# A hybrid block on one core: early loads of attention's keys in the scan's buffers, waits in pieces, another order in the projection

## The reference

```python
h = modulate(x, shift, scale)                     # from the condition vector c
z, xbc, dt, q, k, v, g = split_projection(h @ w_in)
xbc = silu(depthwise_conv_centred(xbc, w, b))     # 5 taps
# branch A: chunked scan (chunks of 128) in both directions, D_INNER = 2048
y = ssd(x*dt, dt*A, B, C) + reversed + d_skip*x ; y = rms_norm(y * silu(z)) @ w_ssd_br
# branch B: 16 query heads, 4 key heads, head size 64; block of 128 queries reads
# 3 blocks of keys (|i-j| <= 128), a sink logit, and all 256 context keys
q, k = apply_rope(q), apply_rope(k)
a = softmax([q.k_window, q.k_context, sink]) @ v ; a = a @ w_attn_br
x = layer_norm(alpha*x + gate * ((sigmoid(g1)*y + sigmoid(g2)*a) @ w_o))
x = layer_norm(alpha*x + gate * experts(x))       # 16 experts, each picks its tokens
```

## Time and profile before

| | value |
|---|---|
| median of 3 runs (lowest, highest) | 2726.47 us (2726.16, 2729.87) |
| profiled execution | 2728.03 us, span 2726.4 us |
| TensorE busy | 2425.6 us, 89% of the span |
| VectorE busy | 1710.5 us, 63% |
| ScalarE busy | 1090.6 us, 40% |
| GpSimd busy | 484.0 us, 18% |
| DMA | 572.02 MB, mean 210 GB/s |
| mean granted clock of TensorE | 0.944 |

### The profile page before, as it was taken

How to read it: one execution, slowest core, us unless ns; L and a number is a source line. 1 busy time by engine, 2 the same in 40 slices (tenths; PEclk the granted TensorE clock), 3 DMA queues, 4 the chain that set the end, 5 groups by cost and what they waited for, 6 DMA issues and landing times. The chain is left out here.

```text
span 2726.4 us, 32819 instructions
## 1 busy us (share of the span) xinstructions
PE 2425.6 (89%) x12804; PEld 1983.2 (73%) x12804; DVE 1710.5 (63%) x1827; ACT 1090.6 (40%) x1363; POOL 484.0 (18%) x385
## 2 busy tenths in 40 slices
PE   7899999989989996894999969999872899999993
PEld 2788888777788885673666659999661788888882
DVE  5555555444234773783565557674666699999996
ACT  3333332221123111551333454442432577777772
POOL 0000000021003432894000000000343011111112
PEclk8899999999999998996999979999895899999996
DMA  5222234576336865976444269978435699999994
GB/s 217 76 77 79 77 125 108 154 233 224 120 114 211 293 250 175 319 264 171 64 75 99 64 186 263 265 212 226 156 116 224 254 381 404 401 400 397 396 382 139
DMA packets 360756, 572.02 MB, mean 210 GB/s; under 512 B 25014, under 2 KB 269206, under 8 KB 337258
## 3 DMA queue, kind: packets, MB, share of 16 engines
q1 hardware_dynamic: 331610, 464.93, 51.2%
q0 software_dynamic: 23376, 97.36, 11.1%
q10 hardware_dynamic: 5632, 7.87, 1.0%
HBM read 460.09 MB, written 104.49 MB: 207 GB/s over the span
## 5 line engine op out<-in xcount | busy, mean ns | idle before, releaser
L2653 DVE TENSOR_TENSOR e_wlo<-e_w,e_whi 128x2048 fp32r<-128x2048 f32 x188 | 425.4, 2289 | 42.4 <-ACT e_whi L2602 41.1
L2602 ACT CAST e_whi<-e_w 128x2048 fp32r<-128x2048 f32 x192 | 365.3, 1909 | 124.0 <-PE e_gu L2779 83.0
L459 PE MATMUL f_lat<-h_hi,w_hi 128*128 128x512 f32 x800 | 255.1, 400 | 20.5 <-DVE w_lo L610 20.5
L459 PE MATMUL f_lat<-h_lo,w_hi 128*128 128x512 f32 x800 | 252.0, 396 | 0.0
L459 PE MATMUL f_lat<-h_hi,w_lo 128*128 128x512 f32 x800 | 251.9, 396 | 0.0
L2113 PE MATMUL b_acc<-b_hi,b_whi 128*128 128x256 f32 x768 | 219.1, 285 | 7.2 <-issue 7.2
L2113 PE MATMUL b_acc<-b_hi,b_wlo 128*128 128x256 f32 x768 | 218.4, 284 | 0.0
L2113 PE MATMUL b_acc<-b_lo,b_whi 128*128 128x256 f32 x768 | 218.4, 284 | 0.0
L459 PEld LDWEIGHTS f_lat<-h_hi,w_hi 128*128 128x128 f32 x800 | 138.1, 189 | 52.3 <-DVE w_lo L610 20.9
L459 PEld LDWEIGHTS f_lat<-h_lo,w_hi 128*128 128x128 f32 x800 | 140.7, 189 | 30.1
L459 PEld LDWEIGHTS f_lat<-h_hi,w_lo 128*128 128x128 f32 x800 | 140.5, 189 | 30.0
(11 more groups left out here) (375 smaller groups left out, 5416.4 us busy)
## 6 DMA issues: line engine op xcount, KB each, us to landing
e_w<-in_w_gate_up SPq DMA_DIRECT2D x128, 1024.0 KB, 11.0
e_w<-in_w_down SPq DMA_DIRECT2D x64, 1024.0 KB, 9.1
w_raw<-in_w_in SPq DMA_DIRECT2D x50, 512.0 KB, 4.0
t_space<-xbcT POOLq DMA_DIRECT2D x18, 1280.0 KB, 6.3
before<-t_space SPq DMA_DIRECT2D x16, 1024.0 KB, 4.5
y_before<-before SPq DMA_DIRECT2D x64, 256.0 KB, 6.2
l_w<-in_w_ssd_br SPq DMA_DIRECT2D x20, 768.0 KB, 7.3
xbcT<-t_out POOLq DMA_DIRECT2D x20, 640.0 KB, 4.4
```

The costliest lines, as they stand in the source:

```text
L459: mm = nc.tensor.matmul(o, weights[:, b, k, :], part[:, k, a:a + n], start=(k == 0 and n_pass == 0), stop=(k == KT - 1 and n_pass == 2))
L2602: nc.scalar.copy(whi[:, slot % SPLIT], w[:, slot]).then_inc(w_hi, 1)
L2653: V.tensor_tensor(wlo[:, slot % SPLIT], w[:, slot], whi[:, slot % SPLIT].bitcast(F32), ALU.subtract).then_inc(w_split, 1)
```

## The change

**Projection.** `keep_lo` of tile n - 1 stands ahead of `rotate_in` of tile n on VectorE. The gates are written into `padded` (their stores read it), without a wait for the low halves. Of `padded` only three strips at the edges are cleared. The last row of modulation is stored ahead of the last gate tile.

**Scan and attention share one space in SBUF** (class `Early`): the scan's three slots are laid out so that keys, queries and masks fit in a slot when its last chunk is done. SyncE issues the loads for attention's first block behind the stores of units 23 to 30. The ones in k2 and the zeros in q2 come by transfer from a constant `flat` of two long rows. Query blocks 1 and 2, with their zeros, are issued by ScalarE at the start of attention. z, y, `decay` and `pre` of the scan lie in buffers of the later stage (class `Later`, now made ahead of the scan; it was made before attention).

**Scan.** The wait for a chunk's tiles is split into four (`bc_in`, `cum_in`, `group_in` with the table, `rows_in` with the lanes). Nothing but the rows of ones is filled, and the matmuls of the exponents read 18 rows. The constants' loads follow the first bc tiles. The last unit's sums and product are made by VectorE. The wait for the stores of y and the `recycle` after the scan are gone; GpSimd waits for the stores in attention, ahead of `load_branch`.

**Attention.** The memset of v is GpSimd's. The maxima of block 0 wait for mask, identity and edges alone, not for all constants. `maximum` writes its sum in place, in PSUM.

The core of the diff:

```diff
 def constants
+        "flat": np.stack([np.zeros(KVH * KV_TOK, np.float32), np.ones(KVH * KV_TOK, np.float32)]),
...
 project_f_stage, sync: store_gate
-                    sp.dma_start(gF[row:row + P, :], wide[:, n % 2, CTX:TOK]).then_inc(gate_out[n % 2], 16)
+                    sp.dma_start(gF[row:row + P, :], padded[:, n % 2, 0:SEQ]).then_inc(gate_out[n % 2], 16)
                 for n in range(NG - 3, NG):
-                    store_gate(n)
                     if n == NG - 1:
                         for c in range(REST):
                             if c not in [SUM_AFTER[k] for k in SUM_AFTER if k + 4 < NG]:
                                 store_rest(c)
+                    store_gate(n)
 scalar: evacuate, gates
-                        act.wait_ge(qk_lo_made, NQK - 1 + b)
-                        nc.scalar.activation(wide[:, b, CTX:TOK], lat[:, b, :], ACT.Sigmoid).then_inc(acc_free, 1)
+                        nc.scalar.activation(padded[:, b, 0:SEQ], lat[:, b, :], ACT.Sigmoid).then_inc(acc_free, 1)
 vector
-                dve.memset(padded[:], 0.0).then_inc(conv_step, 2 * CS)
+                for a, b in ((0, 2), (2 + CTX, 6 + CTX), (PAD - 2, PAD)):
+                    dve.memset(padded[:, :, a:b], 0.0).then_inc(conv_step, 2 * CS // 3)
                 for n in range(1, NQK):
                     split_lo(NX + n + 2, n % 2)
+                    keep_lo(n - 1)
                     rotate_in(NX + n, n % 2, n)
-                    keep_lo(n - 1)
...
+class Early:
+    def load_query(self, eng, part, rows, out, m):
+        at = KV_LAT0 + m * P
+        eng.dma_start(out[rows].bitcast(F32), part[0:QH * HD, :].rearrange("(h d) t -> d h t", d=HD)[:, :, at:at + P]).then_inc(self.q_in[m], 16)
+    def blank(self, s, eng, m):
+        eng.dma_start(self.q2[m][HD:P].bitcast(F32).rearrange("p h q -> p (h q)"), s.flat[0:1, 0:QH * P].to_broadcast([HD, QH * P])).then_inc(self.q_in[m], 16)
+    def load(self, s, eng, qkH, qkL, u):
+        low, high = slice(0, HD), slice(HD, P)
+        if u == 23:
+            self.load_key(eng, qkH, low, self.k1, self.keys_in)
+        if u == 24:
+            self.load_key(eng, qkH, high, self.k1, self.keys_in)
+        if u == 25:
+            self.load_query(eng, qkH, low, self.q1[0], 0)
+            self.load_query(eng, qkL, high, self.q1[0], 0)
+        if u == 26:
+            eng.dma_start(self.mask[0], s.masks[0]).then_inc(self.const_in, 16)
+            eng.dma_start(self.ident, s.squares[:, 0:P]).then_inc(self.const_in, 16)
+            eng.dma_start(self.edge, s.edges[1].rearrange("p (e q) -> p e q", e=2)).then_inc(self.const_in, 16)
+        if u == 27:
+            self.load_key(eng, qkL, low, self.k2, self.keys_in)
+        if u == 28:
+            eng.dma_start(self.k2[high].bitcast(F32).rearrange("p g t -> p (g t)"), s.flat[1:2, :].to_broadcast([HD, KVH * KV_TOK])).then_inc(self.keys_in, 16)
+        if u == 29:
+            self.load_query(eng, qkH, low, self.q2[0], 0)
+            self.blank(s, eng, 0)
+        if u == 30:
+            eng.dma_start(self.mask[1], s.masks[1]).then_inc(self.mask_in, 16)
...
 scan_output_stage, sync
-                sp.dma_start(sq[:], s.squares.rearrange("p (a q) -> p a q", q=P)[:, 0:3, :]).then_inc(const_in, 16)
-                sp.dma_start(dskip[:], s.x["d_skip"].to_broadcast([P, HEADS])).then_inc(const_in, 16)
                 for n in range(NB):
-                    sp.wait_ge(own_ones, n + 1)
                     load_tiles(n)
                 for u in range(UNITS):
                     store(u)
+                    early.load(s, sp, qkH, qkL, u)
                     if u % G == G - 1 and u // G + NB < LCHUNK:
                         load_tiles(u // G + NB)
-                for g in range(G):
-                    sp.wait_ge(y_out[g], 16 * LCHUNK)
 tensor
-                    pe.wait_ge(tiles_in[j], TI * (n // NB) + TI)
+                    pe.wait_ge(bc_in[j], 32 * (n // NB) + 32)
-                pe.wait_ge(const_in, 32)
-                pe.wait_ge(lanes_in, 16 * RB)
 vector, behind the last unit
+                V.tensor_tensor(part[:, b, 0], part[:, b, 0], part[:, b, 1], ALU.add).then_inc(y_last, 1)
+                V.tensor_tensor(pre[:, b], pre[:, b], part[:, b, 0], ALU.add).then_inc(y_last, 1)
+                V.tensor_tensor(y[:, g], pre[:, b], z[j][:, 512 * g:512 * g + 512], ALU.mult).then_inc(y_last, 1)
...
 attention_stage, tensor
-                        pe.wait_ge(q_in[j], 80 * (m // QB) + 48)
-                        if m < QB:
-                            pe.wait_ge(q2_blank, m + 1)
-                        if m == 1:
-                            pe.wait_ge(far_in, 48)
+                        pe.wait_ge(q_in[j], 80 * (m // QB) + 64)
-                pe.wait_ge(near_in, 48)
-                pe.wait_ge(k2_ones, 1)
+                pe.wait_ge(keys_in, 64)
 scalar
                 for m in range(1, QB):
-                    act.dma_start(q1[high, m].bitcast(F32), qL[:, :, q_cols(m)]).then_inc(q_in[m], 16)
+                    early.load_query(act, qkH, low, q1[m], m)
+                    early.load_query(act, qkL, high, q1[m], m)
+                    early.load_query(act, qkH, low, q2[m], m)
+                    early.blank(s, act, m)
 vector: maximum
-                    V.tensor_tensor_reduce(masked[:, h % 2], a_ps[:, h % 2, A0:A0 + KEYS], mask[:, variant(m)], 1.0, NEG,
+                    V.tensor_tensor_reduce(a_ps[:, h % 2, A0:A0 + KEYS], a_ps[:, h % 2, A0:A0 + KEYS], mask[variant(m)], 1.0, NEG,
                                            ALU.add, ALU.max, top[:, h:h + 1]).then_inc(maxed, 1)
 gpsimd
-                G_.memset(k2[HD:P].bitcast(F32), 1.0).then_inc(k2_ones, 1)
-                for j in range(QB):
-                    G_.memset(q2[HD:P, j].bitcast(F32), 0.0).then_inc(q2_blank, 1)
+                G_.memset(v[:], 1.0).then_inc(v_ones, 1)
+                for g in range(GROUPS):
+                    pool.wait_ge(later.y_out[g], 16 * LCHUNK)
 program
-        scan_output_stage(s, xbcT, xbcF, zT, tabs, cumrow, logrow, before, yT)
-        s.recycle()
```

More of the change, by code:

```diff
@@ L1140, in scan_output_stage @@
+def scan_output_stage(s, later, early, qkH, qkL, xbcT, xbcF, zT, tabs, cumrow, logrow, before, yT):
     nc = s.nc
@@ L1335, in merge @@
                         dve.wait_ge(args_made, HALVES * u + half + 1)
-                        V.copy_predicated(arg_ps[:, half, 0], later, arg_ps[:, half, 1]).then_inc(merged, 1)
+                        V.copy_predicated(arg_ps[:, half, 0], above, arg_ps[:, half, 1]).then_inc(merged, 1)
                 def coefficients(n):
@@ L1474, in attention_stage @@
-def attention_stage(s, later, yT, qkH, qkL, vT, aF):
+                    if u + 1 < UNITS:
+                        add_carried(u)
+                        finish(u)
+def attention_stage(s, later, early, yT, qkH, qkL, vT, aF):
     nc = s.nc
@@ L2966, in program @@
         s = Stage(nc, inputs, out, ctx)
[L2967 removed]
+        s.squares, s.cosine, s.sine, s.masks, s.edges, s.lanes, s.flat = (constants[n] for n in ("squares", "cosine", "sine", "masks", "edges", "lanes", "flat"))
         cond_cols, mod = s.scratch("cond_cols", [P, KT]), s.scratch("mod", [1, 6 * D])
@@ L2993, in program @@
                 later = Later(s, st)
-                attention_stage(s, later, yT, qkH, qkL, vT, aF)
+                with ExitStack() as shared:
+                    early = Early(s, shared)
+                    scan_output_stage(s, later, early, qkH, qkL, xbcT, xbcF, zT, tabs, cumrow, logrow, before, yT)
+                    attention_stage(s, later, early, yT, qkH, qkL, vT, aF)
                 branch_stage(s, later, yT, aF, gF, mF)
```

264 lines of the change are left out of this document (141 added, 123 removed).

## The result

The changed kernel takes 2690.65 us (median of 4 runs, 2690.05 to 2690.85) against 2727.22 us of the kernel before on the same chip: ratio 0.9867, 95% interval 0.9852 to 0.9882. It is faster by 36.6 us; 51 were forecast, and the time lies 0.65 us above the range. The profiled execution took 2690.61 us with a span of 2688.9 us, 37.5 us less than before.

The account below looks back on a forecast made before the run. TensorE was taken to bound attention once it runs, full DMA engines its start. Terms 1.4 + 14.5 + 2 + 32.8 (scan and attention together) gave about 51 us off 2726.5, so 2675.5 us; range 2661 to 2690.

Parts of the forecast that it names:

- The tile order: Projection, query and key tiles: the low half ahead of the rotation takes 14.5 us off, bounds 11 and 16.
- rival 4: Projection: swap transfers set the tile period, so reordering does nothing; 37 us off, 2690; chance 0.23 together with Rival 1.
- The clearing: Start of the projection: three strips cleared in place of 2576 columns win 1.4 us, bounds 0 and 2.2.
- The store of modulation: End of the projection: the last modulation row stored ahead of the last gate tile wins 2 us, bounds 0 and 8.
- The scan's start: Start of the scan: SyncE's queue and the first y store move 4.5 us sooner, bounds 2 and 7.
- The scan's end: End of the scan: VectorE making the last unit wins 4 us, the dropped store wait and semaphore clearing 1.6.
- The keys: Start of attention: loads issued early from about 1208, priced at 262 GB/s for long rows, bring first scores at about 1247.5.
- ScalarE: Start of attention: eight transfer issues hold it until 1267.5; it takes up the maxima at 1270.5, 30 us sooner.
- Writing in place: Attention's maxima written to PSUM rather than SBUF: zero effect on the time.
- Behind the first exponential: From attention's first exponential to the kernel's end: no loss of what was saved ahead.
- Rival 1: Start of attention stays with DMA: 20 of 32.8 us won, 38 in all, 2688; chance 0.23 together with rival 4.
- rival 2: More comes off: projection-end gap closes whole (6 more), ScalarE isn't held (3 more); 60 us off, 2666; chance 0.18.

Follow-up runs that it names:

- the run with GpSimd's fills: The changed kernel with the ones and zeros written by GpSimd memsets at attention's start instead of transfers from constant rows; 2680.82 us, ratio 0.9840.
- the 66-row kernels: The changed kernel with maxima in partitions 64 and 65 and second matmul over 66 partitions, 2689.84 us; the same plus two scan edits, 2684.81 us.

## Why the prediction was wrong, step by step

- **The tile order** was right, in mechanism and size: 14.5 forecast, 14.9 measured ((594.08 - 439.23) - (578.72 - 438.79)). The swap transfers don't set the period, so rival 4 fell.
- **The clearing**: 1.4 forecast, 0.44 at the first query copy in this pair of traces. The copy stands at 437.3 to 439.9 us in nine traces with the new start and at 439.2 to 440.6 in five with the old one, 1.1 us apart in the mean, so the term is of the right size and the 0.44 is scatter.
- **The store of modulation** was mis-sized, to the other side: 2 forecast, 7.7 by the gap and 2.8 by the clock behind it (1.2 in the run with this edit alone). I had listed 8 as a bound and taken 2 because a gate store of 512 KB lands in 2.6 us. The trace showed that all engines began within 0.06 us of each other at 757.2, which is a barrier with one last comer, and the mod store was the last thing issued ahead of it. That this miss went the good way is luck: without it the time would have been 8.5 us further above the range. Another 1.65 us is won within the states stage; I can't say why, and the length of that stage differs by 1.6 us between runs of the same code for it.
- **The scan's start**: 4.5 forecast, 3.7 at unit 4, then -0.4 at unit 30. Of the 3.7 a part is scatter: unit 4 stands at 61.5 to 62.7 us in four traces of the scan before and at 59.0 to 60.4 in five of the changed one. The sentence "the same columns: nothing" on the 18 rows failed: 0.23 us a unit, and at the coefficients of five chunks 4.1 us in all, 2.2 of them at one.
- **The scan's end**: 5.6 forecast (last unit, wait and clearing), 0.3 measured from unit 30's finish on. "The issues cannot hold up y much" was beside the point. SyncE's own block ends only when its last issue is out, and the zeros' issue held it 9 us. I had named who waits for the stores and not who waits for SyncE. In the run with GpSimd's fills, where nothing holds it, 4.9 of the 5.6 are there.
- **The keys** is the step that failed most, by the price of its transfers. The first score came 210.3 us into the scan for 194.2. Of these 16.1 us, 4.7 are the lost head start: the first key half went out at 159.4 us, not at 154.7. The other 11.4 are the row of transfers. From the first issue to the first score I had 39.5 us (1208 to 1247.5), the trace has 50.9 (1185.16 to 1236.03). Between them move 8.9 MB for attention's first block and 2.1 MB of y: 11.0 MB in 50.9 us are 216 GB/s (with all that was under way beside them 12.1 MB, 238 GB/s at share 1.04). I had 262 GB/s from a transfer of 0.52 MB, two microseconds long, whose 17 slices of 0.125 us give 247 rather; the start of attention itself, 28 us at 247 GB/s with share 1.05, stood in the earlier trace rows and would have given 44.5. The ones and zeros among them, 2.1 MB, I priced as transfers and still called the exchange for memsets free; the run with GpSimd's fills, which moves 3.1 MB less in all, says 10.9 us.
- **ScalarE** was held by its issues as forecast, until 1257.1, with the values' copy directly behind. It took up the maxima at 1259.8, 3.9 us later than they would have let it (1255.19 and the 0.68 us of the earlier trace rows); 3.2 were forecast. The "2100 open rows" are measured no closer than this: two query parts of 1024 rows each went out in 0.68 and 0.74 us, and the third was held 7.87 us.
- **Writing in place** was right: nothing in the time.
- **Behind the first exponential** I counted no loss. 5.6 us are lost from it to the end: 1.6 up to attention's last maximum, 3.2 from there to the first expert weights (2.2 of them in the residual stage, where transfers are waited for), 0.8 in the experts. In the other runs the whole lies between -1.9 and 6.3 us, apart from the 66-row kernels. Its cause was not tried.

So 9.6 us more than forecast came out of the projection and its end, 17.2 less from scan and attention, and 5.6 were given back. Rival 1 (the start of attention stays with the DMA engines) came true with 15.6 of 32.8 us where it said 20; the first half of rival 2 came true with it. Each had a time; their sum had none. That the time lies only 0.65 us above the range is luck: two misses of 9.6 and 22.8 us stand against each other.

## What to carry to other kernels

Price a long row of transfers by the rate of the longest stretch in which the DMA engines are full, not by a short burst (here 216 to 247 GB/s and 262), and count constants sent in place of memsets as bytes of that row. When an issue may find its queue full, ask who waits for the engine that issues: at the end of a block that is everyone. When several engines start at the same moment after a gap, look for the last small store ahead of it: its size need not tell when it lands.

## What the runs showed of the hardware

- A store of 4 KB from one partition held a barrier for 8.2 us (749.02 to 757.2), where 512 KB from 128 partitions land in 2.6 us; issued one tile earlier, it leaves a gap of 1.8 us.
- In one unit, four matmuls over 18 partitions in place of 128, with the same columns, cost 0.23 us: 0.13 up to the next operation and 0.10 in it.
- Matmuls over 66 partitions in every second place kept TensorE at a granted clock of 0.50 over 18 us of nearly unbroken work (17.5 us busy), in both kernels that have them, where with 128 it was at 0.78 over 16 us, and at 0.85 to 0.90 in five others.
- Loads into 64 partitions each came in at 203 to 233 GB/s with the DMA engines at share 1.03 to 1.19; with the two halves of the keys issued by two engines at once it was 241 GB/s for 223 over 10 us.
- An issue can hold its engine: 0.47 us for the ones, 8.98 us for the zeros issued 5.6 us later behind more transfers.
